# Value units between the modulation groups, odd first tiles on VectorE, and a shifted pairing of modulation units in a two-block transformer kernel

## What is computed

```python
for l in range(DEPTH):
    sh_l, sc_l, g_l = jnp.split(jax.nn.silu(c) @ w_mod[l] + b_mod[l], 3, axis=-1)
    sh_c, sc_c, g_c = jnp.split(jax.nn.silu(c_ctx) @ w_mod[l] + b_mod[l], 3, axis=-1)
    hl = xl * (1.0 + sc_l[:, None, :]) + sh_l[:, None, :]
    hc = xc * (1.0 + sc_c) + sh_c
    ...
    parts_l = jnp.split(hl @ w_in[l], SPLIT_POINTS, axis=-1)
```

## Time and profile before

| | us |
|---|---|
| median of 3 runs | 3125.67 (3123.62 to 3125.68) |
| the profiled execution | 3123.38 |
| its span | 3121.7 |
| PE busy | 2958.1 (95%) |
| DVE busy | 1832.5 (59%) |
| ACT busy | 1286.0 (41%) |
| first product of weight unit 3 begins | 145.80 |

### The profile page before, as it was taken

One profiled execution on the slowest core, in us unless ns is written; L12 is line 12 of the kernel. 1 busy time (PEld: TensorE's weight loads), 2 busy tenths in 40 slices (PEclk: granted clock), 3 DMA queues, 4 the chain that ended last, 5 costly groups with the idle time before them and its releaser, 6 DMA issues.

```text
span 3121.7 us, 41867 instructions
## 1 busy us (share of the span) xinstructions
PE 2958.1 (95%) x15206; PEld 2415.0 (77%) x15206; DVE 1832.5 (59%) x2979; ACT 1286.0 (41%) x1961; POOL 124.5 (4%) x180
## 2 busy tenths in 40 slices
PE   5799999999999979999997999999999999999998
PEld 2477777777777758888886788888788888888886
DVE  1124545454454564777787578777777556565564
ACT  2222323232332243444454545454556535444453
POOL 0000000000000020011101000000000000000000
PEclk7899999999999989999998999999999999999999
DMA  8644334333344323343443444444445455555553
GB/s 340 263 162 151 147 142 156 148 149 143 155 167 180 128 80 119 138 149 133 138 172 121 175 176 153 171 176 162 160 163 200 178 189 185 192 188 194 185 199 122
DMA packets 75567, 518.94 MB, mean 166 GB/s; under 512 B 8736, under 2 KB 11296, under 8 KB 13856
## 3 DMA queue, kind: packets, MB, share of 16 engines
q1 hardware_dynamic: 71296, 505.44, 44.1%
q0 software_dynamic: 2688, 8.91, 0.8%
q10 hardware_dynamic: 1440, 2.60, 0.2%
HBM read 514.82 MB, written 2.10 MB: 166 GB/s over the span
## 4 chain that ended last, share of the span: by engine, by line
PE 87%; DVE 6%; ACT 3%; issue 2%; DMA 1%; ACTq 0%; DVEq 0%; POOLq 0%; POOL 0%
PE bank L1690 23%; PE bank L1693 12%; PE bank L1680 9%; PE bank L1681 8%; PE bank L1682 8%; PE bank L1998 4%; PE bank L1999 4%; PE bank L2000 4%; PE bank L1712 3%; PE bank L1723 3%; PE bank L1713 3%; PE bank L1714 3%; DVE w_lo L992 2%; DVE se L1117 1%; DMA raw<-stream 1%
## 5 line engine op out<-in xcount | busy, mean ns | idle before, releaser
L992 DVE TENSOR_TENSOR w_lo<-raw,w_hi 128x1024 fp32r<-128x1024 f32 x768 | 925.9, 1224 | 662.7 <-ACT w_hi L555 662.1
L555 ACT ACTIVATE w_hi<-raw 128x1024 fp32r<-128x1024 f32 x768 | 806.9, 1056 | 825.5 <-DMA raw<-stream 339.6
L1680 PE MATMUL bank<-x,w_hi 128*128 128x512 f32 x1152 | 461.6, 401 | 4.6 <-DVE x L1041 3.9
L1681 PE MATMUL bank<-x,w_hi 128*128 128x512 f32 x1152 | 453.2, 393 | 0.0
L1682 PE MATMUL bank<-x,w_lo 128*128 128x512 f32 x1152 | 452.7, 393 | 0.0
L1690 PE MATMUL bank<-xs,w_hi 128*128 128x512 f32 x1536 | 394.1, 399 | 13.5 <-DVE xs L1041 13.5
L566 ACT ACTIVATE z<-bank 128x512 f32<-128x512 f32 x272 | 162.8, 599 | 516.4 <-PE bank L1693 276.2
L1690 PEld LDWEIGHTS bank<-xs,w_hi 128*128 128x128 f32 x1536 | 278.7, 190 | 64.8 <-issue 13.9
L1680 PEld LDWEIGHTS bank<-x,w_hi 128*128 128x128 f32 x1152 | 219.0, 190 | 95.7 <-issue 52.0
L1690 PE MATMUL bank<-mlp_x,w_hi 128*128 128x512 f32 x1024 | 257.2, 393 | 0.3 <-DVE w_lo L992 0.3
L1682 PEld LDWEIGHTS bank<-x,w_lo 128*128 128x128 f32 x1152 | 218.9, 190 | 47.4
(11 more groups left out here) (267 smaller groups left out, 3304.5 us busy)
## 6 DMA issues: line engine op xcount, KB each, us to landing
raw<-stream SPq DMA_DIRECT2D x480, 1024.0 KB, 4.8
res<-tokens POOLq DMA_DIRECT2D x8, 512.0 KB, 7.7
work<-tokens POOLq DMA_DIRECT2D x16, 256.0 KB, 6.5
out<-res SPq DMA_DIRECT2D x8, 256.0 KB, 3.1
gain_sb<-final_gain ACTq DMA_DIRECT2D x1, 1024.0 KB, 6.7
table_sb<-tables ACTq DMA_DIRECT2D x1, 640.0 KB, 6.2
pool_sb<-pool_w POOLq DMA_DIRECT2D x8, 64.0 KB, 3.7
work<-lam_in ACTq DMA_DIRECT2D x1, 256.0 KB, 3.0
```

Of the source, the lines that this page charges most:

```text
L555: own.inc(act.activation(w_hi[:, 2 * unit.parity + g, :], raw[:, unit.slot, g * HALF:(g + 1) * HALF], ACT.Copy), hi_done, 2 * unit.number ...
L992: own.inc(dve.tensor_tensor(w_lo[:, n, :], raw[:, unit.slot, g * HALF:(g + 1) * HALF], w_hi[:, n, :].bitcast(F32), ALU.subtract), lo_done, ...
L1680: pe.matmul(bank[:, :], hi, operand[:, k, 0, :], start=k == 0, stop=False)
L1681: pe.matmul(bank[:, :], hi, operand[:, k, 1, :], start=False, stop=False)
```

## The change

1. In the stream, weight units 0 to 3 now stand between the two groups of each round (four modulation units, the weight unit, four modulation units). ACT and DVE split weight unit kq right after the first group's copy and the first group's `modulation`, not after the four tiles.
2. PE multiplies the first half of the previous value unit between a round's first group and that group's collect; the second half stays behind the second collect.
3. Of the first token tiles, DVE scales and shifts the odd ones; ACT only rounds those. A new semaphore `h_odd` carries that.
4. ACT loads `cond`, then `chooser`, then `vectors`; `ident` is loaded after the first phase. PE waits for `chooser` only before its first collect.
5. Units 4 and 5 follow each other in the stream with no modulation unit beside; from unit 6 to unit 65, modulation unit 26 + n goes beside weight unit n. The groups are collected in units 9, 13, 17, ..., 65, which are slots 1, 5 and 9. `PAIRS` is 66, so units 64 and 65 use bank 0 too.
6. Counts of `h_full` start 16 lower, as the first tiles no longer count there.

```diff
-PAIRS = 64
+PAIRS = 66
 def mod_place(u):
-    return 9 * (u // 8) + u % 8 if u < 32 else 2 * u - 28 if u < 92 else u + 74
+    return u + u // 8 + (u % 8 >= 4) if u < 32 else 2 * u - 26 if u < 92 else u + 74
 def weight_place(n):
-    return 9 * n + 8 if n < 4 else 2 * n + 29 if n < PAIRS else n + 92 if n < AHEAD else n + MODS
+    if n < 6:
+        return 9 * n + 4 if n < 4 else n + 32
+    return 2 * n + 27 if n < PAIRS else n + 92 if n < AHEAD else n + MODS
...
             act.dma_start(cond_sb[:], cond).then_inc(cond_in, 16)
+            act.dma_start(chooser[:], squares[:, 2, 0:2]).then_inc(const_in, 16)
             act.dma_start(vec[:], vectors).then_inc(vec_in, 16)
-            act.dma_start(ident[:], squares[:, 0]).then_inc(const_in, 16)
-            act.dma_start(chooser[:], squares[:, 2, 0:2]).then_inc(const_in, 16)
...
                     take_mod(2 * kq + b, b)
+                    if b == 0:
+                        split(Unit(kq))
                 act.wait_ge(mod_done, 2 * kq + 2)
-                for k in range(4 * kq, 4 * kq + 4):
-                    round_first(k, k % 2, k // 2 + 1, reuse=k >= 2)
-                split(Unit(kq))
+                for k in range(4 * kq, 4 * kq + 4, 2):
+                    round_even(k)
+                    act.wait_ge(h_odd, k // 2 + 1)
+                    act.activation(x[:, k + 1, 0, :], h_tmp[1], ACT.Copy).then_inc(xhi_done, 1)
...
-                    if l == 0 and unit.fixed % 4 == 3:
-                        take_mod(7 + unit.fixed // 4, 1)
+                    if l == 0 and unit.fixed % 4 == 1:
+                        take_mod(6 + unit.fixed // 4, 1)
...
                     modulation(2 * kq + b, 4 * kq + KT * b, b)
-                for k in range(4 * kq, 4 * kq + 4):
-                    rest_x(0, k, h_tmp[k % 2], x, WIDE)
-                split(Unit(kq))
+                    if b == 0:
+                        split(Unit(kq))
+                for k in range(4 * kq, 4 * kq + 4, 2):
+                    dve.wait_ge(tok_in, 16 * (k // 2 + 1))
+                    if k:
+                        dve.wait_ge(xhi_done, k)
+                    own.wait_own()
+                    for s in range(2):
+                        cols = slice(TOK * s, TOK * (s + 1))
+                        last = dve.tensor_scalar(h_tmp[1][:, cols], res[:, k + 1, cols], mod[:, KT + k + 1, s:s + 1],
+                                                 mod[:, k + 1, s:s + 1], ALU.mult, ALU.add)
+                    own.inc(last, h_odd, k // 2 + 1)
+                    rest_x(0, k, h_tmp[0], x, WIDE)
+                    rest_x(0, k + 1, h_tmp[1], x, WIDE)
...
             pe.wait_ge(cond_full, 1)
-            pe.wait_ge(const_in, 16 * 2)
...
                         mod_product(8 * kq + 4 * b + q, b)
+                    if kq and b == 0:
+                        value_half(Unit(kq - 1), 0, kq - 1, v_banks[0], 0, x)
+                    if kq + b == 0:
+                        pe.wait_ge(const_in, 16)
                     mod_collect(2 * kq + b, b)
-                    if kq:
-                        value_half(Unit(kq - 1), b, kq - 1, v_banks[0], 0, x)
+                    if kq and b == 1:
+                        value_half(Unit(kq - 1), 1, kq - 1, v_banks[0], 0, x)
...
-                group = 7 + n // 4
-                if n % 4 == 0:
+                group = 8 + (n - 6) // 4
+                if n % 4 == 2:
                     pe.wait_ge(mod_done, group)
-                mod_product(28 + n, 1)
-                if n % 4 == 3:
+                mod_product(26 + n, 1)
+                if n % 4 == 1:
                     return lambda: mod_collect(group, 1)
```

More of the change, by code:

```diff
@@ L315, in two_blocks @@
         h_full = sem("h_full")
+        h_odd = sem("h_odd")
         xhi_done = sem("xhi_done")
@@ L593, in values @@
                     split(Unit(first + n))
-                if l == 0:
-                    take_mod(8, 1)
                 split(Unit(first + 9))
@@ L620, in take_mod, with round_even @@
                 own.inc(act.activation(z[:, b, :], gemm_bank[b][:, :], ACT.Copy), modz_full, group + 1)
-            def round_first(k, b, loaded, reuse=True):
-                act.wait_ge(tok_in, 16 * loaded)
-                if reuse:
+            def round_even(k):
+                act.wait_ge(tok_in, 16 * (k // 2 + 1))
+                if k:
                     act.wait_ge(x_full, k - 1)
@@ L628, in round_first @@
                     cols = slice(TOK * s, TOK * (s + 1))
-                    last = act.activation(h_tmp[b][:, cols], res[:, k, cols], ACT.Identity,
+                    last = act.activation(h_tmp[0][:, cols], res[:, k, cols], ACT.Identity,
                                           scale=mod[:, KT + k, s:s + 1], bias=mod[:, k, s:s + 1])
-                own.inc(last, h_full, k + 1)
+                own.inc_own(last)
                 own.wait_own()
-                act.activation(x[:, k, 0, :], h_tmp[b], ACT.Copy).then_inc(xhi_done, 1)
+                act.activation(x[:, k, 0, :], h_tmp[0], ACT.Copy).then_inc(xhi_done, 1)
             act.wait_ge(cond_in, 16)
@@ L650, in _ @@
             act.dma_start(mean_w[:], squares[:, 1]).then_inc(rope_in, 16)
+            act.dma_start(ident[:], squares[:, 0]).then_inc(rope_in, 16)
             values(0)
@@ L752, in norm @@
                     if l == 1:
-                        act.wait_ge(h_full, 16 + k + 1)
+                        act.wait_ge(h_full, k + 1)
                         act.activation(xs[:, k, 0, :], h, ACT.Copy).then_inc(xhi_done, 1)
@@ L802, in _ @@
             for k in range(KT):
-                if k in (3, 7):
-                    take_mod(21 + k // 4, 1)
+                if k in (1, 5, 9):
+                    take_mod(20 + k // 4, 1)
                 slot(Unit(W_OUT0 + k))
@@ L897, in after @@
                     def after():
-                        act.wait_ge(h_full, 32 + k + 1)
+                        act.wait_ge(h_full, 16 + k + 1)
                         act.activation(mlp_x[:, k, 0, :], h_tmp[j % 2][:, 0:TOK], ACT.Copy).then_inc(xhi_done, 1)
@@ L912, in after @@
                         def after():
-                            act.wait_ge(h_full, 48 + 16 * c + k + 1)
+                            act.wait_ge(h_full, 32 + 16 * c + k + 1)
                             act.activation(hidden[:, k, 0, :], h_tmp[0][:, 0:TOK], ACT.Copy).then_inc(xhi_done, 1)
@@ L1062, in values @@
                     split(Unit(first + n))
-                if l == 0:
-                    modulation(8, 2 * KT, 1)
                 split(Unit(first + 9))
@@ L1213, in after @@
                             own.inc(dve.tensor_tensor(y, att[4][:, 0:t_y], y, ALU.mult), ot_used, hh + 1)
-                    if l == 0 and unit.fixed % 4 == 3:
+                    if l == 0 and unit.fixed % 4 == 1:
                         inner = before
                         def before():
-                            group = 7 + unit.fixed // 4
+                            group = 6 + unit.fixed // 4
                             modulation(group, 4 * group, 1)
@@ L1346, in two_tiles @@
                             own.inc(dve.tensor_scalar(h_buffer(l, q, b), res[:, k + b, 0:TOK],
-                                                      vcol("norm_mix_g", k + b), None, ALU.mult), h_full, 16 + k + b + 1)
+                                                      vcol("norm_mix_g", k + b), None, ALU.mult), h_full, k + b + 1)
                 for pair in range(KT // 2):
@@ L1384, in before @@
                 def before():
-                    if k in (3, 7):
-                        group = 21 + k // 4
+                    if k in (1, 5, 9):
+                        group = 20 + k // 4
                         modulation(group, 4 * group, 1)
@@ L1564, in after @@
                         own.inc(dve.tensor_scalar(h, res[:, k, 0:TOK], vcol("norm_mlp_g", k), None, ALU.mult),
-                                h_full, 32 + k + 1)
+                                h_full, 16 + k + 1)
                         rest_x(7, k, h, mlp_x, TOK)
@@ L1597, in epilogue @@
                             own.wait_own()
-                            own.inc(dve.memset(tiny[:, 62:63], 0.0), h_full, 48 + 16 * c + k + 1)
+                            own.inc(dve.memset(tiny[:, 62:63], 0.0), h_full, 32 + 16 * c + k + 1)
                             return dve.memset(tiny[:, 61:62], 0.0)
@@ L1772, in values @@
                     unit = Unit(first + 4 + kq)
-                    halfway = mod_beside(unit.fixed) if l == 0 else None
+                    halfway = mod_beside(unit.fixed) if l == 0 and kq >= 2 else None
                     for g in range(2):
@@ L1866, in _ @@
                 unit = Unit(W_OUT0 + k)
-                halfway = mod_beside(unit.fixed) if k < 8 else None
+                halfway = mod_beside(unit.fixed) if unit.fixed < PAIRS else None
                 product(unit, "wide", 1, x, halfway)
```

3 lines of the change are left out of this document (2 added, 1 removed).

## The result

| | us |
|---|---|
| before, median of 4 | 3124.64 (3123.22 to 3125.68) |
| changed, median of 4 | 3081.55 (3077.12 to 3084.93) |
| ratio | 0.9859, 95% interval 0.9847 to 0.9872 |
| profiled execution of the changed kernel | 3077.12, span 3075.2 |

The change takes 43 us off by the medians, 1.4%. Between the two profiled executions it is 46.3 (3123.38 - 3077.12). The forecast was 3085, from 3068 to 3102.

The account below looks back on a forecast made before the run. PE was taken as the bound from 145.8 us, a chain of waits before that. Gains of 26.3 (second-phase stalls) and 14.1 (first phase) sum to 40.4 off 3123.4, 3083.0; plus 2.3 for the median, 3085, range 3068 to 3102.

Parts of the forecast that it names:

- The stalls of the second phase: Collects moved to slots 1, 5, 9 no longer wait behind the softmax: 14.0 of waiting plus 12.3 of clock, 26.3 us.
- I take zero: Second phase: the collects' new places in slots 1, 5 and 9 were taken to cost nothing.
- The first phase: Up to the first unit of the second phase: starts at 144.5 instead of 158.56, a gain of 14.1 us.
- Start: First phase: earlier chooser and PE freeing slots as units land recover 3.0 us of missing transfer; first tiles at 34.7.
- Rounds: First phase: each round takes 30.3 us against 33.2; three bring the last mod_done to 125.6, now 136.85.
- the walk: First phase: step-by-step sum along the new round, from one second mod_done to the next, 30.3 us.
- Rest: From the last mod_done to the second phase's first unit: 18.9 us instead of 21.7.
- A: Rival: the clock stays up in the first phase, 15.4 us together, 3070 us; chance 13%.
- B: Rival: first-phase rounds gain nothing, as the second value half holds PE while slots fill; 3096 us; chance 15%.
- C: Rival: second-phase stalls only move, PE waiting in slots 5 as now in slot 3; 3112 us; chance 5%.
- D: Rival: slower, ACT's copy or DVE's modulation late in each of the fifteen new collects; 3190 us; chance 4%.
- the rule on loads: First-phase 1 MiB loads: measured 4.80 us used, not the skill's estimated 4.4, which would make the time 1 us less.

Follow-up runs that it names:

- e1: Kernel before with only the shifted pairing (collects in slots 1, 5, 9), first phase untouched: 3099.3 us, ratio 0.9921.
- e3: Kernel before, pairing untouched, with ACT's copy for the collect in slot 3 moved ahead of the softmax of slot 2: 3097.8 us, ratio 0.9916.
- e7: Changed kernel with vectors, ident and chooser loaded in the old order and PE waiting for both tables before its first product: 3088.3 us, ratio 0.9890.
- e4: Changed kernel with PE's collect of each first group ahead of the value half again: 3071.8 us, ratio 0.9830.
- e5: Changed kernel with DVE's split of the weight unit ahead of the first group's modulation, PE's order kept: 3073.4 us, ratio 0.9838.
- e9: e4 with the weight unit two places earlier in the stream and its split ahead of the group's copy and modulation: 3078.2 us, ratio 0.9857.
- e11: e4 run again, on the same chip as a repeat of the changed kernel: 3070.92 us, ratio 0.9828.
- e12: Changed kernel with the edits of e4 and e5 both: 3068.70 us, ratio 0.9825.
- e6: Changed kernel with ACT scaling and shifting all four first tiles of a round, as before the change: 3083.7 us, ratio 0.9873.

## Why the prediction was right

**The stalls of the second phase: right, in mechanism and size.** The term was 26.3: 14.0 of waiting and 12.3 of clock. The output product's first matmul began at 892.59 before and begins at 845.14 in the changed kernel:

```profile
892.59 0.47 PE L1680 MATMUL bank<-x,w_hi 128*128 128x512 f32 x1 [3.88 <-DVE x L1041]
...
845.14 0.47 PE L1694 MATMUL bank<-x,w_hi 128*128 128x512 f32 x1 [3.73 <-DVE x L1045]
```

That is 47.45 us earlier. 2.8 of them are work not yet done (two modulation products and one collect, which now come behind this point), 18.1 came from the first phase, which leaves 26.6. `e1` and `e3` show the cause. "I take zero" for the new places holds too: none of their collects waits. ACT's slack was read rightly (in the first slot 5 the copy ends at 254.36, the collect begins at 258.63). DVE's was not: 2.4 us were forecast, and the thinnest place, in a slot 1, has 0.8:

```profile
701.00 0.22 DVE L1037 TENSOR_TENSOR mod<-bank,vec 128x4 f32<-128x4 f32 x2
...
702.04 1.06 PE L1737 MATMUL bank<-raw,cond_x 128*32 128x512 f32 x8
```

So this place cost nothing with little to spare.

**The first phase: right in mechanism, low in size**, 14.1 against 18. *Start*: 3.0 was forecast and 2.2 came (the second modulation at 35.27, was 37.46):

```profile
37.46 0.23 DVE L1033 TENSOR_TENSOR mod<-bank,vec 128x4 f32<-128x4 f32 x2 [14.15 <-PE bank L1731]
```

That looks close and was put together from two things that I had not told apart: with the old tables but the new stream it is 39.98 (`e7`). So the weight unit in the middle of round 0 cost 2.5 and the tables gave 4.7, and in the end they are worth 6.7, more than twice the term. *Rounds*: 30.3 was the walk, 28.1 to 29.8 came. In the round shown, the value half behind the second collect took 6.9 instead of 8.03, since full clock came back 2.8 us into it and not 5.3, and the first collect with its modulation 1.06 instead of 1.36. That is most of the 1.65. *Rest*: 18.9 was the walk, 18.2 came (122.2 to 140.4). By part, the start fell short by 0.8, the three rounds brought 4.2 more than the walk (86.7 us against 90.9) and the rest 0.7 more.

**A gain that was not in the sum**: 1.7 us. Behind 893 us the kernel before had one more stretch at half clock, for 3.4 us; the changed kernel has none there. That this belongs to the change is not shown, and the runs speak against it: PE's wait ahead of this place is 3.73 to 3.88 us in all thirteen profiled executions, and the matmuls behind it ran at half clock in ten of them. `e4`, `e5`, `e7`, `e9` and `e11` are among the ten, though their second phase is that of the changed kernel; only the changed kernel's two executions and `e12` stayed at full clock. What decides it is open.

**The sum**: 40.4 by the forecast; 46.3 between the profiled executions, 43.1 between the medians; the profiled execution was the fastest of the changed kernel's four. The parts above, 18.1, 26.6 and 1.7, account for the 46.3. Behind the start of the output product the kernels with the new pairing are alike, and their profiled executions take between 2230.1 and 2234.1 us there; a difference of 3 us between forecast and medians is within that.

**Rivals.** A (full clock in the first phase) did not come, at a mean clock of 0.80, though the half-clock stretch in the value half of the round shown is shorter. B was half right: its mechanism, the load behind the weight unit waiting for the value half, was there and in the walk's sum, and was worth 8 to 11 us as `e4` and `e5` show; but it only ate into the gain. C and D did not come, D with less to spare than the earlier trace rows let expect. The tiles are hidden as argued (`e6`).

**By the rule on loads**: in the changed kernel the loads on the chain that are issued into idle engines take 4.73, 4.75 and 4.79, as the row of before did (4.76, or 4.80 up to the next step); the term stays with the row. The Trainium skill (DMA: Bandwidth & Descriptors, "Anatomy of one DMA — SWDGE (gpsimd) path") gives its 2.0 us plus bytes over 436 GB/s for DMAs that GpSimd issues. The loads here are issued by SP, so the 4.4 is not a figure for them, and no run here has a load of 1 MiB issued by GpSimd.

## What to carry to other kernels

A wait has to be priced with what follows it: here 3.5 us of waiting cost another 3.5 in three cases of four and 1.8 in the fourth, since the matmuls behind ran at half clock. It is a price that can fall due and need not: behind the wait of 3.7 to 3.9 us ahead of the output product the clock was halved in ten profiled executions and not in three. When one engine's copy releases the bottleneck, look at what stands ahead of it in that engine's own order; two moved lines (`e3`) were worth as much as a new pairing of the whole stream. In a ring of few slots, lay out the round as one chain and ask which step holds a slot: moving the release (DVE's split ahead of a small add) gave 8 us, and moving the unit itself (`e9`) took 6 of `e4`'s gain away.

## What was not expected of the hardware

One 1 KiB table kept the start of the kernel: `chooser`, issued fourth at 2.28 us behind a stream of 1 MiB loads, landed 13.4 us later, while `cond`, issued first, took 5.3. In the changed kernel `chooser` is issued second, at 1.32, and lands 8.6 us later; PE no longer waits for it ahead of its first product and starts at 7.1. The earlier issue and the later wait together (with `ident` moved away) were worth 6.7 us in a kernel of 3080, of which I can account for 3.4 as idle transfer time. Which of the two brings it was not tried.
